# Grid attention: reciprocals multiplied into the probabilities before they are turned, and three shared key blocks of 128 for the outer column groups

## What is computed

```python
def neighborhood_attn(q, k, v, rpb):
    rows = S // GRID_W                     # 16 rows of 64 columns
    kr = min(NA_ROWS, rows)                # 8 key rows for each query row
    cs = jnp.clip(col - NA_COLS // 2, 0, GRID_W - NA_COLS)
    colmask = (col[None, :] >= cs[:, None]) & (col[None, :] < cs[:, None] + NA_COLS)
    ...
    def one(r):
        rs = jnp.clip(r - kr // 2, 0, rows - kr)
        ...
        s = jnp.einsum('bqhd,bikhd->bhqik', qblk, kblk).astype(jnp.float32) * scale + bias
        s = jnp.where(colmask[:, None, :], s, -jnp.inf)
        p = jax.nn.softmax(s.reshape(B, H, GRID_W, kr * GRID_W), axis=-1)
        ...
        return jnp.einsum('bhqik,bikhd->bqhd', p, vblk)
...
y = jnp.concatenate([yc, ym], axis=-1) * jax.nn.silu(gate)
x = x + y @ w_out_odd[o]
```

## Time and profile before

| | us |
|---|---|
| median of 3 runs | 2340.4 (2339.95 to 2343.82) |
| the profiled execution's own time | 2340.63 |
| its span, first to last instruction | 2338.9 |
| PE busy | 2257.0, 96% of the span |
| DVE busy | 1584.3, 68% |
| ACT busy | 1305.0, 56% |
| POOL busy | 683.1, 29% |
| mean granted TensorE clock | 0.997 |

### The profile page before, as it was taken

One profiled execution on the slowest core, in us unless ns is written; L12 is line 12 of the kernel. 1 busy time (PEld: TensorE's weight loads), 2 busy tenths in 40 slices (PEclk: granted clock), 3 DMA queues, 4 the chain that ended last, 5 costly groups with the idle time before them and its releaser, 6 DMA issues.

```text
span 2338.9 us, 35387 instructions
## 1 busy us (share of the span) xinstructions
PE 2257.0 (96%) x11778; PEld 1918.3 (82%) x11778; DVE 1584.3 (68%) x3262; ACT 1305.0 (56%) x3054; POOL 683.1 (29%) x843
## 2 busy tenths in 40 slices
PE   7999999999999999999999999899999999999999
PEld 6888888888888878888888888787787888887887
DVE  7444677677886433346655566658888878889787
ACT  6444566666775444446565566655656645465542
POOL 3455232311235642222222222565563200000000
PEclk9999999999999999999999999999999999999999
DMA  7322101111233342322322322633343633345734
GB/s 229 116 76 60 41 28 37 32 35 48 62 121 109 99 136 68 95 68 86 95 85 80 95 87 88 193 91 117 100 145 108 202 96 95 109 151 167 231 116 137
DMA packets 332356, 241.69 MB, mean 103 GB/s; under 512 B 66448, under 2 KB 284816, under 8 KB 331664
## 3 DMA queue, kind: packets, MB, share of 16 engines
q1 hardware_dynamic: 332176, 239.43, 33.6%
HBM read 195.59 MB, written 43.78 MB: 102 GB/s over the span
## 4 chain that ended last, share of the span: by engine, by line
PE 81%; DVE 9%; ACT 4%; issue 3%; DMA 1%; POOL 1%; SPq 1%; DVEq 0%; ACTq 0%; POOLq 0%
PE PS L1943 15%; PE PS L1945 15%; PE PS L1944 15%; PE PS L2176 6%; PE PS L2177 6%; PE PS L2178 6%; PE PS L2092 5%; PE PS L2059 5%; PE PS L2045 2%; PE PS L2046 2%; ACT PY L2187 1%; PE PS L2101 1%; PE PS L2000 1%; DVE ST L2555 1%; PE PS L2083 1%
## 5 line engine op out<-in xcount | busy, mean ns | idle before, releaser
L2852 POOL TENSOR_TENSOR WS<-WR,WS 128x256 fp32r<-128x256 f32 x635 | 493.4, 798 | 990.9 <-ACT WS L2187 990.1
L1943 PE MATMUL PS<-HT,WS 128*128 128x512 f32 x1492 | 602.5, 404 | 18.2 <-POOL WS L2852 6.2
L1945 PE MATMUL PS<-HT,WS 128*128 128x512 f32 x1492 | 584.0, 391 | 0.0
L1944 PE MATMUL PS<-HT,WS 128*128 128x512 f32 x1492 | 582.3, 390 | 0.0
L1943 PEld LDWEIGHTS PS<-HT,WS 128*128 128x128 f32 x1492 | 281.2, 188 | 76.6 <-issue 12.2
L1945 PEld LDWEIGHTS PS<-HT,WS 128*128 128x128 f32 x1492 | 280.7, 188 | 61.6
L1944 PEld LDWEIGHTS PS<-HT,WS 128*128 128x128 f32 x1492 | 281.7, 189 | 52.0
L2187 ACT ACTIVATE WS<-WR 128x256 fp32r<-128x256 f32 x658 | 245.3, 410 | 90.1 <-PE PS L1945 57.7
L2187 ACT ACTIVATE PT<-PS 128x512 fp32r<-128x512 f32 x352 | 186.2, 529 | 193.5 <-PE PS L2059 192.9
L2445 DVE TENSOR_TENSOR PT<-PS,PT 128x512 fp32r<-128x512 f32 x352 | 211.1, 609 | 84.5 <-ACT PT L2187 81.5
L2092 PE MATMUL PS<-PT,QKV 128*128 128x256 f32 (+3 forms) x1248 | 207.8, 288 | 3.5 <-DVE YB L2624 2.4
(11 more groups left out here) (284 smaller groups left out, 4554.9 us busy)
## 6 DMA issues: line engine op xcount, KB each, us to landing
WR<-in_w_in_odd SPq DMA_DIRECT2D x106, 256.0 KB, 2.9
EO<-in_grid SPq DMA_DIRECT2D x48, 384.0 KB, 3.1
WR<-in_ffn_in SPq DMA_DIRECT2D x60, 256.0 KB, 2.9
WR<-in_w_in_even SPq DMA_DIRECT2D x100, 128.0 KB, 2.5
WR<-in_w_out_odd SPq DMA_DIRECT2D x48, 256.0 KB, 2.8
yd<-PY SPq DMA_DIRECT2D x44, 256.0 KB, 3.3
EO<-in_ffn_in SPq DMA_DIRECT2D x35, 256.0 KB, 3.1
WR<-in_w_in_even SPq DMA_DIRECT2D x34, 256.0 KB, 2.9
```

The lines of the kernel that those rows point to most:

```text
L1943: e.matmul(out, wh, rh, start=start, stop=False)
L1944: e.matmul(out, wh, rl, start=False, stop=False)
L1945: return e.matmul(out, wl, rh, start=False, stop=stop)
L2852: e.tensor_tensor(ws(i, 1, n), RAW[raw_slot(u)][:, o:o + n], f32(ws(i, 0, n)), ALU.subtract).then_inc(s_wlop.sem, 1)
```

## The change

Four things, in chunks of kind "c" only (`EARLY = ("c",)`).

1. A new step "divide": DVE multiplies a score's probabilities (128x384, in place) by their reciprocal and 0.5. Both "recip" steps and both "divide" steps of job k-1 are put ahead of job k's scores. The transposes of job k-1 wait for `s_div`.
2. "finish" has no spread any more: PE transposes nothing, DVE does not multiply the gate, and the copy to `RW` is gone.
3. In outer groups both scores now span the same three blocks of 128 keys (16 rows of 24 columns), so that all three blocks are shared; the score's matmuls still cover 11 or 12 rows, but mask, exp and divide run over 384 columns instead of 288.
4. The values of outer groups are laid out in blocks of 128 keys. The middle block's upper half comes from the second half of the projection, so "flip v" of that half has one more instruction of 64x128 on ACT and on DVE (`v_edge`).

```diff
+EARLY = ("c",)
...
+        def divide(job):
+
+            for s in job.scores:
+                recip(s)
+            for s in job.scores:
+                s.divided = s_div.add()
+                put("divide", s)
...
-            if job:
+            if job and not job.c.early:
                 for s in job.scores:
                     recip(s)
...
                     job = pend["job"]
+                    if job and job.c.early:
+                        divide(job)
                     s0 = score(c, pp, h, 0)
...
-                return Chunk(12 + i, 1, i, kind, j, slot, (j + 1) % 2, lambda t: (t % 2, 288 if t // 2 in (0, 3) else 384),
+                return Chunk(12 + i, 1, i, kind, j, slot, (j + 1) % 2, lambda t: (0 if t // 2 in (0, 3) else t % 2, 384),
...
+        def v_edge(i):
+
+            src = PS[64:128, B_X, 256 * i:256 * i + 128].rearrange("p (h c) -> p h c", h=2)
+            o = 1536 * i + 256
+            v = v_grid(0)[64:128, o:o + 256].rearrange("p (h x c) -> p h x c", h=2, x=2)
+            return src, v[:, :, 0, :], v[:, :, 1, :]
...
                     w.wait_ge(s_exp, job.scores[1].no)
+                    if job.c.early:
+                        w.wait_ge(s_div, job.scores[1].divided)
...
-                                    o = 512 * job.pp + 256 * (k % 2) + 128 * h
-                                    vv = v_grid(k // 2)[0:job.tile, o:o + 128]
+                                    n, z = ((0, 0), (0, 1), (1, 1))[k] if job.pp in (0, 3) else (k // 2, k % 2)
+                                    o = 512 * job.pp + 256 * z + 128 * h
+                                    vv = v_grid(n)[:, o:o + 128]
...
                     f, = of
+                    if f.c.early:
+                        until[B_O] = (s_fin, f.y if f.c.mem else f.fin + 2)
+                        continue
                     w.wait_ge(s_rec, f.rec)
...
+                elif kind == "divide":
+                    s, = of
+                    p, rd = p_at(s.c, s.slot, 0, s.nk), RD[:, s.pp % 2, s.x, s.h:s.h + 1]
+                    w.wait_ge(s_rec, s.rec)
+                    e.tensor_scalar(p, p, rd, 0.5, ALU.mult, ALU.mult).then_inc(s_div.sem, 1)
...
-                    w.wait_ge(s_spread, f.no)
                     w.wait_ge(s_ed, max(c.gate) if c.grid else c.gate[f.pp // 2])
-                    e.scalar_tensor_tensor(out=sg, in0=spread, scalar=0.5, in1=sg, op0=ALU.mult, op1=ALU.mult).then_inc(s_fin.sem, 1)
+                    if not c.early:
+                        w.wait_ge(s_spread, f.no)
+                        e.scalar_tensor_tensor(out=sg, in0=spread, scalar=0.5, in1=sg, op0=ALU.mult, op1=ALU.mult).then_inc(s_fin.sem, 1)
```

More of the change, by code:

```diff
@@ L100, in __init__ @@
         self.fins = []
-    def tile(self, pp):
-        return 96 if self.grid and pp in (0, 3) else 128
 class Score:
@@ L123, in __init__ @@
         self.c, self.pp, self.h, self.scores = c, pp, h, (s0, s1)
-        self.tile = c.tile(pp)
-        self.span = [range(c.keys(t)[0], c.keys(t)[0] + c.keys(t)[1] // self.tile) for t in (2 * pp, 2 * pp + 1)]
+        self.span = [range(c.keys(t)[0], c.keys(t)[0] + c.keys(t)[1] // 128) for t in (2 * pp, 2 * pp + 1)]
         both = [k for k in self.span[0] if k in self.span[1]]
@@ L548, in flip @@
             vt = s_flip.add()
-            put("flip v", h, i, vt, s_ea.add(), s_ed.add(), free)
+            both = 2 if h.kind == "vg" and h.n == 1 else 1
+            put("flip v", h, i, vt, s_ea.add(both), s_ed.add(both), free)
             return s_flip, vt
@@ L772, in recip @@
             s.spread, s.before = spread_at[s.pp % 2], s_spread.n
-            s.wide = s.x == 1 and s.h == 1
+            s.wide = s.x == 1 and s.h == 1 and not s.c.early
             s_rec.add(1 if s.wide else 0)
@@ L2056, in tensor_program @@
                         for z, x in enumerate(who):
-                            n = job.tile
-                            p0 = n * (k - job.span[x][0])
-                            m = e.transpose(PS[0:n, B_PT + pb, o + 128 * z:o + 128 * z + 128], p_at(job.c, job.scores[x].slot, p0, p0 + n), ID[:, :])
+                            p0 = 128 * (k - job.span[x][0])
+                            m = e.transpose(PS[:, B_PT + pb, o + 128 * z:o + 128 * z + 128], p_at(job.c, job.scores[x].slot, p0, p0 + 128), ID[:, :])
                     m.then_inc(s_turn.sem, 1)
@@ L2078, in tensor_program @@
                             out = PS[:, B_O, 256 * h + 128 * who[0]:256 * h + 128 * who[0] + n]
-                            p = PT[0:job.tile, pb, part, o:o + n]
+                            p = PT[:, pb, part, o:o + n]
                             a, b = first and z == 0 and part == 0, final and z == len(job.banks[i]) - 1 and part == 1
@@ L2264, in scalar_program @@
                     act(hi, src, scale=1.0).then_inc(s_ea.sem, 1)
+                    if h.kind == "vg" and h.n == 1:
+                        src, hi, _ = v_edge(i)
+                        act(hi, src, scale=1.0).then_inc(s_ea.sem, 1)
                 elif kind == "rope 1":
@@ L2520, in vector_program @@
                     take(lo, src, hi).then_inc(s_ed.sem, 1)
+                    if h.kind == "vg" and h.n == 1:
+                        src, hi, lo = v_edge(i)
+                        take(lo, src, hi).then_inc(s_ed.sem, 1)
                 elif kind == "rope 1":
@@ L3084, in grid_tables @@
             r, c = (i.reshape(-1, 1) for i in np.mgrid[8 * g:8 * g + 8, q0:q0 + 16])
-            kr, kc = (i.reshape(1, -1) for i in np.mgrid[4 * g:4 * g + 12, k0:k0 + wide])
+            r0, rows = (4 * g, 12) if wide == 32 else (0, 16)
+            kr, kc = (i.reshape(1, -1) for i in np.mgrid[r0:r0 + rows, k0:k0 + wide])
             rs, cs = np.clip(r - 4, 0, 8), np.clip(c - 8, 0, 48)
```

30 lines of the change are left out of this document (16 added, 14 removed).

## The result

The changed kernel took 2510.28 us (median of 4 runs, 2506.93 to 2514.03) against 2342.11 for the kernel before (2339.95 to 2344.01): a ratio of 1.0719, 95% interval 1.0699 to 1.0739, so 168 us slower. The forecast was 2478 with a range of about 2440 to 2550. The profiled execution took 2509.35 us, its span is 2507.5, its mean granted clock 0.971 (before 0.997).

What follows compares the result with a forecast made beforehand. The prediction took PE to set the pace in the grid chunks; stalls 127 less savings 15.4 plus clock 27 gave 139 us on 2340.4, so 2479, stated as 2478, range about 2440 to 2550.

Steps and rivals of the forecast that it cites:

- PE is the bound and waits for nothing else: In the grid chunks PE was busy 61.93 of 62.00 us, so work removed or waits added count in full.
- Work taken from PE, 15.4 us: Outer groups' values with two matmuls for four, 7.7 us, and no transposes of RW, 7.7 us.
- Stalls, 127 us in some 50 waits: In the grid stage, PE waits for DVE's divides before a job's first transpose: 14 over 3 us, 36 of 1 to 3.
- the subtraction of mask start less transpose start: Per job, how late DVE reaches the divides without new work; 0.95 us per wait was added for reciprocals and divides.
- sized at 0.3 us each: Extra 64x128 instructions in second-half "flip v", two such flips ahead of divides per chunk; 0.6 us a chunk.
- The divide at 0.39 us, by the copy's slope: One DVE divide of 384 elements, taken from an SBUF copy's 0.62 ns an element; upper bound 0.56 us.
- The clock, 27 us: PE's clock falls after stalls in the grid stage: 1.3 us for 14 long waits, 1 us for a quarter of 36.
- The first rival: Clock falls at nearly every stall, 85 us instead of 27: 2537 us, or 2557 with the dear divide; chance 0.17.
- Stalls of half the size: Waits on PE pull other things forward, so grid-stage stalls are half: about 2402 us; chance of smaller stalls 0.16.
- Faster: DVE reaches the divides in time, so only PE's 15.4 us count: 2325 us; chance 0.04.
- Gate to gate: The way from one gate's mask to the next gate's, 56.3 us before, becomes about 75 us.

Runs made afterwards that it cites:

- e9: As e7, but with the kernel before's four key blocks of 96 and no extra flip instruction; 2337.71 us, ratio 0.9984 to the kernel before.
- e7: The changed kernel with divides right behind the job's own exps, ahead of the next leave, and the group's finish behind them; 2336.44 us, ratio 0.9979 to before.
- e11: The changed kernel's divides in their place and no spread, but the old four blocks of 96 and no v_edge; 2498.04 us, ratio 1.0664 to before.
- e1: The changed kernel with reciprocals and divides moved behind the job's own exps, ahead of the next leave in DVE's queue; 2343.21 us, ratio 1.0006 to before.
- e3: The changed kernel with useless 128x512 matmuls filling most of PE's waits for the divides in chunks 5 to 9; 2472.98 us, ratio 1.0558 to before.

## Why the prediction held, and where it was off

- **PE is the bound and waits for nothing else.** Right: all new idle time is at one line, and e9, where the spread, the gate multiply and the RW copy are gone, gains no more than PE's own work (7.0 us).
- **Work taken from PE, 15.4 us.** A little too much. Two values matmuls take 0.32 us, so two in place of four save 0.16 us and not 0.24: the 0.12 us of one matmul in a group of four does not carry over to a group of two. Why is not shown. A job's stretch from the first values matmul to the projection is 1.27 us in e7 against 1.47 in the earlier trace rows and the row behind it, and its scores take 0.01 more: 0.19 saved, 6.1 us in 32. The spread, 0.23 by 32, is 7.4 (e9: 7.0). Together 13.5.
- **Stalls, 127 us in some 50 waits.** Right: 51 waits, 135.8 us, of which about 12 replace idle time of before; PE's idle time as a whole rose by 123.8. The longest is 6.7 us, in the last chunk, where DVE has other work ahead of the divides; the forecast had 4.3, which is right for the steady chunks. In the steady chunk the subtraction of mask start less transpose start, plus 0.95, gave 4.28, 4.27, 1.79, 0, 2.05, 2.41, 1.57 and (gate) 1.40; measured were 4.28, 4.25, 2.50, none, 2.04, 2.38, 2.18 and 1.39. The two that are off are v_edge's, sized at 0.3 us each: they lie 0.71 and 0.61 us above the subtraction, and fall by 0.74 in e11. ACT's instruction and then DVE's lie one behind the other in the chain, 0.3 and 0.33 us.
- **The divide at 0.39 us, by the copy's slope.** Right: 0.40 to 0.42 alone, 0.66 for two from start to start and 0.19 for the reciprocals. The mean of all 128, 491 ns, holds the overlaps with GpSimd, of which the forecast had none. At the change's place 26 of 128 are overlapped, some only at their end; in e1's place 106.
- **The clock, 27 us: the term that failed.** Measured 168.6 - 123.8 + 13.5 = 58.3 us over the span; in the grid stage (119.5 - 6.8) / 2 = 56, or 48 if only the low time in which PE worked is counted (101.5 against 6.3 us). Most of the 10 us between 48 and 58 lie outside the stage, where nothing is changed: 24 us at 0.50 against 7 before, 8 us of time. e3 recovers 37 us by matmuls alone. The forecast counted one fall for each of 14 long waits and one for every fourth of 36 short ones, 23 in all. That was nearly right: of the 26 low stretches one lies at each of the 14 waits of 2.9 us and more, and one at each of 12 of the 37 shorter. What was wrong is the price of one, 1.3 and 1.0 us, taken from a single stretch of 3.3 us: nine stretches at long waits last 6.8 us and the other 17 last 3.4, 4.6 us on average or 2.3 of time, of which 0.35 are idle time. The distance from 2478 to 2510 is this term: 31 us more here, less 3 of waits, and 2 of savings that did not come. The waits and the savings came out as forecast and not by errors that cancel.
- **The first rival**, the clock falling at nearly every stall for 85 us: two thirds of its price, but not its mechanism, since 25 of the 51 waits have no low stretch. The page that was cited for it (the Trainium skill, "TensorE: Matmul & The Clock Gate", section "HAM oscillation — how this bites in real kernels") tells of bursts shorter than the waits between them, each of which restarts at the low clock. Here the work between waits is longer than the waits, and the trace agrees only in part: a low stretch at each of the 14 long waits, but at 12 of the 37 shorter ones.
- **The other rivals.** Stalls of half the size: refuted, each wait is there at its size in every steady chunk. Faster: refuted for this place in the queue, and its condition, the divides ahead of the leave, is what e1 and e7 made true: e7 is at 2336, not at the 2325 that PE's savings alone would give, because of the 2 us that these are smaller and of the clock (10 us).
- **Gate to gate** (seven of a chunk's eight jobs) was to be about 75 us. The masks stand at 1190.41 and 1269.54 on DVE's timeline of after: 79.1. The waits in it are 17.6 us, as read; with these and the 1.7 us that PE saves the 79.1 leave 6.9 us for the clock, where 3 to 4 were put.

## What to carry to other kernels

Where one engine paces the kernel, price a new dependency by when the other engine gets to it in its queue, not by its length: subtract two start times from the trace of before. Halving the divide's length (one column) gave back 36 us of 168, moving it ahead of the leave gave back 167. When waits break up a stretch without idle time, price the falls of the matmul clock too: here they cost 0.47 us for each 1 us of new idle time. And an instruction added on two engines that hand to each other counts with the sum of both.

## What the runs showed of the hardware

- **Falls of the clock.** In the kernel after 12 low stretches of 3.4 us lie at short waits in runs of short matmuls: 11 at waits of 1.95 to 2.4 us, one behind waits of 1.23 and 1.05. They begin between 0.2 us before the end of the wait and 1.6 us after it; the window 1259.20 to 1262.60 above is one, behind a wait of 2.38 us. It is not certain at any such wait: the same wait of 2.04 us has a low stretch in five chunks and none in two. e1's usual wait of 0.94 us has none; of its 5 low stretches (27 us) in the stage four lie at waits of 2.1 to 3.9 us, and one in the first chunk, near where before has its own.
- **VectorE is slowed beside GpSimd.** A copy or a multiplication by a scalar of 128x384, SBUF to SBUF, takes 0.34 to 0.42 us alone and mostly 0.89 to 0.97 beside GpSimd's tensor multiplication; the mask, which reads PSUM, takes 0.55 either way. That all the forms reach much the same length, and that they keep their short one where GpSimd's starts well behind their own start (0.40 us for the divide, 0.34 for the copy), looks like waiting for a turn rather than sharing. The Trainium skill ("SBUF — State Buffer", section "Who interferes with whom") states this as an exclusive lock on a shared port pair; the runs agree, and its cost here is about 0.5 us an instruction.
- **A scalar from memory costs 0.06 us.** The same multiplication takes 0.35 us with two constants and 0.41 with the reciprocal read from SBUF and one constant.
